# GpSimd instead of VectorE divides the attention probabilities by their sums, in a fused decoder layer

## The reference

```python
scores = jnp.where(mask[None, :, None, None], scores, -jnp.inf)
m = jnp.maximum(scores.max(axis=-1), sink)
e = jnp.exp(scores - m[..., None])
probs = e / (e.sum(axis=-1) + jnp.exp(sink - m))[..., None]
o = jnp.einsum('bnkgqs,bnskd->bnqkgd', probs.astype(v.dtype), vb)
return o.reshape(b, s, H * HD) @ wo
```

## Time and profile before

| | |
|---|---|
| median of 3 runs | 1077.31 us (1076.98 to 1077.50) |
| the profiled execution | 1077.67 us, its span 1074.3 us |
| attention, blocks 0 to 7 | from about 31 us to about 276 us of the span |
| granted TensorE clock | 1.00 in all 40 slices of the span |
| PE busy over the span | 1057.5 us (98%) |
| DVE, ACT, POOL busy | 782.0, 472.7, 163.1 us (73%, 44%, 15%) |

### The profile page before, as it was taken

How to read it: one execution, slowest core, us unless ns; L and a number is a source line. 1 busy time by engine, 2 the same in 40 slices (tenths; PEclk the granted TensorE clock), 3 DMA queues, 4 the chain that set the end, 5 groups by cost and what they waited for, 6 DMA issues and landing times.

```text
span 1074.3 us, 13753 instructions
## 1 busy us (share of the span) xinstructions
PE 1057.5 (98%) x4936; PEld 876.7 (82%) x4936; DVE 782.0 (73%) x1127; ACT 472.7 (44%) x819; POOL 163.1 (15%) x270
## 2 busy tenths in 40 slices
PE   7899999999999999999999999999999999999998
PEld 5788888877888888888888888888888888888887
DVE  6877777888445599776677668376776878747985
ACT  6566666676323234313232342353333334437451
POOL 8655555443000000000000000000000000001000
PEclk9999999999999999999999999999999999999999
DMA  8111111050332325253344154998988898660102
GB/s 313 45 34 41 40 40 36 25 196 20 122 114 86 109 87 208 118 196 133 148 170 154 81 193 180 382 412 284 290 294 289 285 334 292 248 234 1 40 30 88
DMA packets 67472, 171.79 MB, mean 160 GB/s; under 512 B 5200, under 2 KB 5456, under 8 KB 67280
## 3 DMA queue, kind: packets, MB, share of 16 engines
q1 hardware_dynamic: 67408, 170.95, 44.3%
HBM read 133.18 MB, written 37.75 MB: 159 GB/s over the span
## 4 chain that ended last, share of the span: by engine, by line
PE 89%; DVE 6%; POOL 2%; issue 2%; ACT 1%; ACTq 0%; POOLq 0%; DVEq 0%
PE pair L2520 28%; PE pair L2500 22%; PE pair L2248 10%; PE pair L2385 8%; PE pair L2566 7%; PE pair L2315 3%; PE pair L2458 3%; PE pair L2283 3%; PE pair L2595 2%; PE pair L2294 1%; PE pair L2428 1%; POOL bias L846 1%; PE pair L2267 1%; DVE qT L1561 1%; PE pair L2227 0%
## 5 line engine op out<-in xcount | busy, mean ns | idle before, releaser
L2520 PE MATMUL pair<-uT 128*128 128x512 f32 x1344 | 305.7, 389 | 0.0
L2520 PEld LDWEIGHTS pair<-uT 128*128 128x128 f32 x1344 | 252.0, 188 | 52.3
L1297 ACT ACTIVATE uT<-wo_raw 128x1024 fp32r<-128x1024 f32 x83 | 84.6, 1054 | 112.6 <-PE pair L2520 96.5
L1951 DVE TENSOR_TENSOR uT<-wo_raw,uT 128x1024 fp32r<-128x1024 f32 x83 | 98.5, 1221 | 44.4 <-ACT uT L1297 43.8
L791 POOL TENSOR_SCALAR row_var<-row_ssq 128x1 f32<-128x1 f32 x16 | 4.0, 249 | 706.2 <-ACT hn L1338 623.0
L2385 PE MATMUL pair<-WA,oT 128*128 128x512 f32 x384 | 90.4, 393 | 1.4 <-DVE WA L1708 1.0
L2385 PEld LDWEIGHTS pair<-WA,oT 128*128 128x128 f32 x384 | 71.2, 188 | 16.9 <-issue 2.4
L2500 PE MATMUL pair<-WA,WB 128*128 128x512 f32 x336 | 78.2, 389 | 0.4 <-ACT xr L1272 0.4
L2500 PEld LDWEIGHTS pair<-WA,WB 128*128 128x128 f32 x336 | 63.0, 188 | 13.8 <-DVE WB L1885 0.8
L2566 PE MATMUL pair<-WA 128*128 128x512 f32 x288 | 68.1, 391 | 0.0
L2566 PEld LDWEIGHTS pair<-WA 128*128 128x128 f32 x288 | 53.7, 188 | 11.0
(11 more groups left out here) (241 smaller groups left out, 1876.7 us busy)
## 6 DMA issues: line engine op xcount, KB each, us to landing
wo_raw<-in_m_w SPq DMA_DIRECT2D x71, 512.0 KB, 6.3
wo_raw<-hid_kept SPq DMA_DIRECT2D x41, 512.0 KB, 5.7
hid_kept<-RES SPq DMA_DIRECT2D x32, 512.0 KB, 2.7
emb<-in_m_w SPq DMA_DIRECT2D x17, 512.0 KB, 5.9
RES<-in_m_w SPq DMA_DIRECT2D x8, 1024.0 KB, 6.6
uT_f<-in_m_w SPq DMA_DIRECT2D x6, 1024.0 KB, 6.8
RES<-in_a_wqkv SPq DMA_DIRECT2D x10, 512.0 KB, 8.4
emb<-hid_kept SPq DMA_DIRECT2D x10, 512.0 KB, 5.6
```

What stands on the lines that cost most here:

```text
L1297: nc.scalar.activation(operand(t, which, HI), unit(t, which), ACT.Copy).then_inc(op_hi, 1)
L1951: nc.vector.tensor_tensor(operand(t, which, LO), unit(t, which), operand(t, which, HI).bitcast(F32), ALU.subtract).then_inc(op_ready, 1)
L2520: mm = nc.tensor.matmul(ps[4 * (j % 2) + m][:], operand(t, 0, s)[:, k, m * P:(m + 1) * P], operand(t, 1, r)[:, k, :], start=(g == 0 and k ...
```

## The change

GpSimd now scales the probabilities, head by head (four instructions of 128x128 in place of one of 128x512), with the reciprocal as a per-partition scalar; `scale_probs` leaves DVE's list and is put into GpSimd's. The order of GpSimd's list in `body` changes with it.

```diff
+            def scale_probs(n, j):
+                pool.wait_ge(rden_ready, 4 * n + j + 1)
+                for r in range(G):
+                    row = probs[:, j % 2, r, 0:P]
+                    scaled = pool.tensor_scalar(row, row, rden[:, j % 2, r:r + 1], 1.0, ALU.mult, ALU.mult)
+                scaled.then_inc(probs_ready, 1)
...
             def body(n, last=False):
-                head_norm("q8", n)
+                if last:
+                    head_norm("q8", n)
+                scale_probs(n, 0)
+                if not last:
+                    head_norm("q8", n)
                 place_sinks(n, 1)
                 mask_probs(4 * n - 1)
...
                 place_sinks(n, 2)
                 dv_hi_part(n)
+                scale_probs(n, 1)
                 mask_probs(4 * n)
...
                     head_norm("k", n + 1)
+                scale_probs(n, 2)
                 mask_probs(4 * n + 1)
                 if not last:
                     place_sinks(n + 1, 0)
+                scale_probs(n, 3)
                 mask_probs(4 * n + 2)
...
                 if j == 0:
                     place_sinks(0, 2)
+                    scale_probs(0, 0)
                 if j == 1:
                     x_norm(1)
                     scale_x(2)
                     dv_hi_part(0)
                     place_sinks(0, 3)
+                    scale_probs(0, 1)
                     mask_probs(0)
...
                     head_norm("k", 1)
+                    scale_probs(0, 2)
                     mask_probs(1)
                 if j == 3:
+                    scale_probs(0, 3)
                     mask_probs(2)
...
-            def scale_probs(n, j):
-                t, i = 4 * n + j, j % 2
-                dve.wait_ge(rden_ready, t + 1)
-                nc.vector.tensor_tensor(probs[:, i, :, 0:P], probs[:, i, :, 0:P],
-                                        rden[:, i, :].unsqueeze(2).to_broadcast([P, G, P]),
-                                        ALU.mult).then_inc(probs_ready, 1)
...
                 invert(n, j)
-                scale_probs(n, j)
```

## The result

The changed kernel takes 1095.69 us (median of 5, 1094.10 to 1097.24) against 1077.24 us (5 runs): 1.0173 times as long, 95% interval 1.0159 to 1.0187. Forecast: 1098, range 1088 to 1108. The profiled execution has a span of 1092.6 us against 1074.3, 18.3 us more.

The account below looks back on a forecast made before the run. PE was taken to bound the kernel, without gaps in blocks 1 to 6. Block 0's 2.0, blocks 1 to 6's 6.0 and block 7's 12.5 summed to 20.5 us more, predicting 1098 us, range 1088 to 1108.

Parts of the forecast that it names:

- The scaling's price: Four GpSimd row instructions per group, estimated from the bias tile: 1.73 us, bounds 1.43 and 4.6.
- Norm of q8: Blocks 1 to 6: queued behind scaling (n, 0), it makes PE wait 0.70 us before project("k"), 0.41 with 1.43 us scaling.
- Norm of q0: Blocks 1 to 6: scaling (n, 1) ahead of mask 4n delays this norm and PE's transpose; 0.3 us (0 to 0.7).
- Norm of k: Blocks 1 to 6: k_var 0.5 us earlier without DVE's multiply, scores(n+1, 0) on time, but nothing gained because of the q8 wait.
- Blocks 1 to 6 together: Sum of the norm delays in the middle blocks: 1.0 us per block, six blocks, 6.0 us (2.5 to 9).
- Block 0: Two scalings ahead of mask 0 delay weigh_values(0, 0) by 1.0 and the norm of q0 behind it: 2.0 us (1 to 3).
- Block 7: Last block: masks queued behind scalings that wait for late reciprocals hold PE's weigh_values; 12.5 us (10.5 to 14).
- rival A: PE slows to half clock after its block 7 gaps, up to +3 us at each of two: 1101 to 1104; chance 0.22.
- closed rings: Block 7 after turn_probs(7, 1): transpose, exps, reciprocal, scaling, previous mask, half of weigh_values, next transpose; 7.9 us each, 8.4 the first.
- Rival B: Middle blocks hide the change with 1.43 us scaling and wider margins; only block 7 and part of block 0 pay: 1090; chance 0.12.
- C: Contention: GpSimd rows cost 1.15 us each, slowing each q8 norm and block 7 scaling by 2.9 us: 1126; chance 0.08.
- D: DVE's relief wins: mask 28 does not hold PE, block 7's 1.3 us wait goes: 1074; chance 0.03.

Follow-up runs that it names:

- the run with the filled gaps: Changed kernel plus 38 unread identity transposes in the middle of weigh_values(7, 0) and of weigh_values(7, 2), ahead of the mask wait: 1092.04 us.
- The reordering run: Against GpSimd scaling in blocks 0 to 6 only (1079.98 us): in blocks 1 to 6 the q8 norm stands ahead of scaling (n, 0) again; 1077.24 us.
- the run with one multiply: Against GpSimd scaling in blocks 0 to 6 only, changed kernel's order: one 128x512 multiply by broadcast reciprocals replaces four 128x128 ones; 1076.57 us.
- the runs with the norm first: GpSimd scaling with the q8 norm ahead of scaling (n, 0) in blocks 1 to 6: 1077.24 us with block 0 on GpSimd, 1076.03 with it on VectorE.
- the runs with the masks first: Block 7's masks ahead of the scalings they were queued behind: 1082.53 us as the changed kernel's only edit, 1074.88 us in the last version.
- the last version: GpSimd scales blocks 1 to 6, q8 norm first, and (7, 0) to (7, 2), masks first; VectorE scales block 0 and (7, 3): 1074.88 us.

## Why the prediction was right

The forecast (1098, slower) held, with 18.4 us measured against 20.5 summed. The places and the waits were right; the total came so close by luck. Most terms were too large, and a rival's mechanism, the clock, which the sum left out, made up 3.6 us of it. At the full clock the kernel takes about 1092 us, as the run with the filled gaps does: still in the range, but 6 us below the forecast. Term by term:

- **The scaling's price**, 1.73 us, was the mis-sized term that runs through all others. The instruction itself is as estimated, 372 ns (0.37), but I put a gap of 0.08 between two, as the bias rows have. Here four take 1.41 in all, from start to start 0.35, which is just under the lower bound of 1.43. The bias rows each signal a semaphore and here only the fourth does; that this makes the difference no run shows.
- **Norm of q8**: 0.70 us per block forecast with 1.73, 0.41 with 1.43, in six blocks. Measured with 1.41: PE comes 0.42 to 0.50 late and the period grows by 0.32 or 0.33, in blocks 2 to 4 (and 5, see the end). The reordering run shows the cause, and the run with one multiply shows that it hangs on the length. Block 1 has no such wait, and block 6 grows by 0.13 only.
- **Norm of q0**: 0.3 us forecast, none measured in blocks 1 to 6. `q_var` starts 3.33 us ahead of PE's transpose (137.10, 140.43), as before (135.32, 138.64): before, the low mask had to wait 0.50 us for DVE's low part; after, GpSimd comes later and finds it done. I had not taken that wait off.
- **Norm of k**: right, down to 0.27 us, and right that it gains nothing while q8's wait takes it back: GpSimd's scaling of (3, 0) starts 5.30 us after `scores(3, 0)` (124.50 - 119.20), and by the rows before it would have been 5.15 (123.06 - 117.91). That it gains 0.17 per block once that wait is gone, the runs with the norm first show.
- Blocks 1 to 6 together: 6.0 forecast, 1.76 measured, below the lower end of 2.5.
- **Block 0**: 2.0 forecast, 1.08 measured. The mask was done at 49.41, not 50.2: the two scalings take 1.42 and 1.58, the value copy 0.41 and not 0.85 without DVE's multiply beside it, and the low mask does not wait for DVE. PE's wait for the mask is 0.19 us, not 1.0; what block 0 pays is 0.49 on `qn`, with the norm of q0, behind it.
- **Block 7**: 12.5 forecast; 14.62 + 0.95 = 15.6 measured, of which 3.6 are the clock (rival A), so 12.0 at the full clock. The mechanism was as forecast, mask 28 behind a late reciprocal and then closed rings, but that 12.0 came out near 12.5 is again luck: the steps were off both ways and cancel.

| more than before, us | forecast | changed kernel | gaps filled |
|---|---|---|---|
| scores(7, 0) to turn_probs(7, 1) | 6.4 | 7.6 | 5.1 |
| to turn_probs(7, 2) | 2.5 | 1.7 | 1.7 |
| to turn_probs(7, 3) | 3.6 | 5.3 | 4.8 |
| to the end | 0 | 0.95 | 0.4 |

In the first step mask 28 was ready 19.9 us after `scores(7, 0)` (at 256.6), not 21.3 (255.3 - 234.01). The ring for (7, 3) took 10.05 us, not 8.3, since its scaling was 2.0 us longer beside the `wo_lo` units, where I had 0.4, and the clock was low again. The lower end of 10.5 for this block does not follow from its reason either: four scalings 0.30 shorter leave 11.3, and 10.9 without the 0.4.

- **Rival A** happened: the granted clock was 0.50 after the gap, and it cost 2.5 us at the first gap and 0.6 + 0.6 around and after the second, where I had put up to 3 each. The rule on the idle array in the Trainium skill's page "TensorE: Matmul & The Clock Gate", section "What's actually happening", agrees with that trace. I gave it 0.22, too little for gaps three times as long as any in the block before. I weighed it with block 7's gap of 1.30 us alone; the same trace has one of 2.34 us ahead of `scores(0, 0)`, with the clock at 1.00 after it, and the last section shows that other executions lose the clock there.
- **Rival B** (the middle blocks hide it) was nearer to blocks 1 to 6 than the forecast was. **C** (contention in all groups) is out, with a median of 372 ns; three of the 32 groups were longer than 1.43 us: (0, 1) with 1.58, (6, 3) with 2.45 and (7, 3) with 3.41. **D** needs that mask 28 does not hold PE, which only the runs with the masks first bring about.

The rule of "SBUF — State Buffer", section "Who interferes with whom", in the Trainium skill held at both ends: `k_var` at 0.27 once DVE's multiply is gone, and 3.41 us for a scaling beside DVE instructions with two SBUF inputs. That block 7's scalings all meet such instructions did not hold: those of (7, 0) to (7, 2) took 1.41 or 1.42.

## What to carry to other kernels

When work moves to another in-order queue, cost what stands behind its wait, not only its duration: the four groups of block 7 cost 15.6 us for 7.7 us of GpSimd's instructions, since a mask that PE needed was queued behind a reciprocal that came late, and moving that mask up took some 13 us back. Check first and last blocks by themselves; the steady blocks hid nearly all of it. A wait of several microseconds on PE can be dearer than it is long, since the clock may fall with it: here 3.6 us on top, for two waits of 4.4 and 4.6 us.

## What the runs showed of the hardware

- The clock falls and rises differently from execution to execution. PE stands 2.3 us shortly before `scores(0, 0)`, at 29 to 31 us, in every profiled execution. In those of before, the changed kernel and the last version the clock was 1.00 over 31 to 34 us; in the other seven it was 0.50 to 0.72. In the one with the masks first it was 0.59, and `scores(0, 1)` started at 38.24 instead of 36.63. That is 1.6 us there and 1.1 by `scores(1, 0)`, and it explains why blocks, not ends, were compared above. It does not hang on an edit: of the 33 runs of the kernel before beside the last four experiments, 17 have a mean clock of 1.000 (median 1076.24 us) and 16 one of 0.998 (median 1077.28), and the profiled executions at 0.998 are those with the low clock there. The window 31 to 34 us of the run with the masks first, columns as in the clock table above:

```profile
31.00:34.00 3.00, 2.95 (x12) 2.66 (x13) 2.72 (x4) 1.16 (x2) 0.00 (x0) 0.59 0.00 0
```

- On GpSimd one 128x512 multiply of two tensors (1.04 us) is shorter than four 128x128 multiplies by a per-partition scalar (1.41 us). VectorE took 0.73 us on average for the same multiply.
- Open: block 5 is 0.3 us longer than its neighbours (29.68 against 29.34) in the changed kernel and in the other runs with four-row scaling in blocks 0 and 1 to 6, but not where block 0 stayed on VectorE or one multiply was used. The first thing late in it is VectorE's `add_bias(5, 2)`, at 19.25 us of the block against 18.99 in block 4, after 0.19 us of standing that no other engine's result ends. Every run in which GpSimd scales in block 0 has this standing in block 5, also the one with one multiply, whose period is no longer there; the others do not have it. No run was made to find out why.
